# Retention heads: strips of one head between the attention steps of the former, key tiles from token 0, values centred by token

## The reference

```
k = k * RET_DK ** -0.5                       # 4 heads, RET_DK = 128, RET_DV = 256
scores = einsum(qc, kc) * intra              # intra[i, j] = gamma_h ** (i - j) where i >= j, else 0
out = einsum(scores, vc) + einsum(qc * q_decay, state)
ret = head_layer_norm(out)                   # over the 256 values of a head:
#   mu = mean(y); var = mean((y - mu) ** 2); (y - mu) * rsqrt(var + EPS)
ret = ret * silu(rg)
merged = g0 * (ret @ w_branch[0]) + g1 * (diff @ w_branch[1]) + g2 * (conv @ w_branch[2])
```

## Time and profile before

| | |
|---|---|
| median of 3 runs | 2200.36 us (2197.75 to 2200.51) |
| span of the profiled execution | 2196.6 us |
| TensorE busy | 2150.5 us (98%) |
| VectorE busy | 1150.0 us (52%) |
| ScalarE busy | 776.6 us (35%) |
| GpSimd busy | 51.3 us (2%) |
| chain that ended last | TensorE 93%, VectorE 4%, ScalarE 2% |

### The profile page before, as it was taken

One profiled execution on the slowest core, in us unless ns is written; L12 is line 12 of the kernel. 1 busy time (PEld: TensorE's weight loads), 2 busy tenths in 40 slices (PEclk: granted clock), 3 DMA queues, 4 the chain that ended last, 5 costly groups with the idle time before them and its releaser, 6 DMA issues.

```text
span 2196.6 us, 33725 instructions
## 1 busy us (share of the span) xinstructions
PE 2150.5 (98%) x13184; PEld 1851.5 (84%) x13184; DVE 1150.0 (52%) x1719; ACT 776.6 (35%) x1214; POOL 51.3 (2%) x79
## 2 busy tenths in 40 slices
PE   9999998999999999999999999999999989999998
PEld 8988994677888778888888888999999988889896
DVE  6553332443555645535445665457755556546365
ACT  4222221332344533323223466333433333222233
POOL 0000000000000000000000000012200000000000
PEclk9999999999999999999999999999999999999999
DMA  4232220132222132223222221231123222222222
GB/s 148 93 105 95 86 86 20 58 106 95 74 72 68 58 126 96 92 96 101 90 96 95 83 92 58 86 118 59 54 103 128 94 77 77 95 87 96 96 87 96
DMA packets 52966, 194.66 MB, mean 89 GB/s; under 512 B 6896, under 2 KB 7280, under 8 KB 52224
## 3 DMA queue, kind: packets, MB, share of 16 engines
q1 hardware_dynamic: 49248, 177.56, 24.6%
q10 hardware_dynamic: 2656, 12.41, 1.5%
q0 software_dynamic: 960, 3.24, 0.5%
HBM read 186.77 MB, written 6.42 MB: 88 GB/s over the span
## 4 chain that ended last, share of the span: by engine, by line
PE 93%; DVE 4%; ACT 2%; issue 1%; DMA 0%; DVEq 0%; ACTq 0%; SPq 0%
PE ps L1797 75%; PE ps L2356 5%; PE ps L2223 1%; PE ps L2013 1%; PE ps L2038 1%; PE ps L1972 1%; PE ps L1957 1%; PE ps L2288 1%; PE ps L2129 1%; DVE kk_r L1441 1%; PE ps L2052 1%; ACT kk L715 0%; ACT kk L716 0%; PE ps L2266 0%; PE ps L2110 0%
## 5 line engine op out<-in xcount | busy, mean ns | idle before, releaser
L406 ACT ACTIVATE wh<-wraw 128x1024 fp32r<-128x1024 f32 x330 | 348.2, 1055 | 834.4 <-PE ps L1797 725.5
L975 DVE TENSOR_TENSOR wl<-wraw,wh 128x1024 fp32r<-128x1024 f32 x330 | 403.4, 1223 | 144.9 <-ACT wh L406 138.0
L1797 PE MATMUL ps<-xh,wh 128*128 128x264 f32 (+1 forms) x2088 | 392.2, 333 | 9.7 <-ACT wh L406 5.7
L1797 PE MATMUL ps<-xh,wl 128*128 128x264 f32 (+1 forms) x2088 | 385.9, 330 | 0.0
L1797 PE MATMUL ps<-xl,wh 128*128 128x264 f32 (+1 forms) x2088 | 385.8, 330 | 0.0
L1797 PEld LDWEIGHTS ps<-xh,wh 128*128 128x128 f32 x2088 | 315.9, 189 | 51.8 <-ACT wh L406 4.6
L1797 PEld LDWEIGHTS ps<-xh,wl 128*128 128x128 f32 x2088 | 316.3, 188 | 38.2
L1797 PEld LDWEIGHTS ps<-xl,wh 128*128 128x128 f32 x2088 | 316.3, 188 | 38.2
L1797 PE MATMUL ps<-bh,wh 128*128 128x264 f32 (+1 forms) x1296 | 234.3, 325 | 3.9 <-DVE hf L1008 1.7
L1797 PE MATMUL ps<-bl,wh 128*128 128x264 f32 (+1 forms) x1296 | 230.9, 322 | 0.0
L1797 PE MATMUL ps<-bh,wl 128*128 128x264 f32 (+1 forms) x1296 | 230.6, 322 | 0.0
(11 more groups left out here) (420 smaller groups left out, 2030.1 us busy)
## 6 DMA issues: line engine op xcount, KB each, us to landing
wraw<-weights_dram SPq DMA_DIRECT2D x331, 512.0 KB, 3.5
hf<-tables_dram POOLq DMA_DIRECT2D x12, 264.0 KB, 3.0
res<-x_t_dram SPq DMA_DIRECT2D x4, 528.0 KB, 7.4
res<-x_t_dram ACTq DMA_DIRECT2D x1, 2112.0 KB, 9.1
res_dram<-res ACTq DMA_DIRECT2D x1, 2112.0 KB, 7.7
mrg_dram<-mrg ACTq DMA_DIRECT2D x1, 2112.0 KB, 7.3
mrg<-mrg_dram ACTq DMA_DIRECT2D x1, 2112.0 KB, 10.6
res<-res_dram ACTq DMA_DIRECT2D x1, 2112.0 KB, 16.5
```

Of the source, the lines that this page charges most:

```text
L406: nc.scalar.activation(wh[:, slot], wraw[:, slot], ACT.Copy).then_inc(hi_done, 1)
L975: nc.vector.tensor_tensor(wl[:, slot], wraw[:, slot], wh[:, slot].bitcast(F32), ALU.subtract)\
L1797: last = nc.tensor.matmul(o, w[:, slot, c, :], a[:, c, tok], start=(k == 0), stop=(k == len(steps) - 1))
```

## The change

- TensorE, VectorE and ScalarE each get one loop written out over 24 strips (`N_RET`) and what follows them. Head h's attention steps stand ahead of the strips 4h + 4 to 4h + 7: `scores`, then the turns of its two value strips and the sum of the former head's squares, then the products for each half. For head 3 these are gate strips.
- Weights come in that order: q, k and two v strips of a head, then the gates. q strips are over 512 tokens.
- Key tiles are tokens 0 to 127, and so on, with the last 16 as a fifth tile: 512, 400, 272, 144 and 16 queries.
- Values are centred once per token in `vt` (`centred_values`) ahead of the products, so outputs have mean 0: the mean matmuls and the subtraction on the outputs go. ScalarE squares straight from PSUM, VectorE adds the two squares, and one matmul sums them.
- Banks: strips 1 to 3 have banks 2 to 7; later ones over 528 tokens have banks 0 and 1, over 512 bank 0 or 1 by parity. `scores` use banks 2 to 4, the turns the same banks afterwards, products banks 5 and 6, the sum bank 7.
- Gates stay in `qq` till all heads are done, then silu, gating and parts follow within the last slots (`ret_silu`, `ret_gated`, `ret_parts`). The weight parts of the first `w_branch` strip of `ret_out` are made ahead (`ahead=True`).

The diff, cut:

```diff
+        RSTRIP, N_RET = START["ret_qkv"], 4 * RH + KC
+        def ret_width(j):
+            return SEQ if j >= 4 * RH or j % 4 == 0 else T
+        def ret_bank(j):
+            return 2 * j if 0 < j < 4 else j % 2 if ret_width(j) == SEQ else 0
+        def first_query(t):
+            return max(P * t - NM, 0)
+        def scores_ap(t):
+            return (ps[:, 2, :], ps[:, 3, 0:400], ps[:, 4, 0:272], ps[:, 4, 272:416], ps[0:NM, 4, 416:432])[t]
+        ret_silu = {21: (0, 1, 2), 22: (3, 4, 5), 23: (6,), 24: (7,)}
+        ret_gated = {22: (0, 1, 2), 23: (3, 4), 24: (5, 6), 25: (7,)}
+        ret_parts = {23: (0, 1, 2), 24: (3, 4), 25: (5, 6), 26: (7,)}
...
 ScalarE
+            for i in range(N_RET + 3):
+                if i <= N_RET:
+                    n = RSTRIP + i + 1
+                    split_hi(n, n // 2, n % 2)
+                h, step = divmod(i - 4, 4)
+                if step == 1 and 0 <= h < RH:
+                    for v in range(2):
+                        f = RDV * h + P * v
+                        act.wait_ge(vtr_done, 2 * h + v + 1)
+                        nc.scalar.activation(vt[:, 0:4, f:f + P], ps[:, 2 + v, :]..., ACT.Copy)
+                        act.wait_ge(vtr_done, 2 * h + 2)
+                        nc.scalar.activation(vt[0:NM, 4, f:f + P], ps[0:NM, 4, P * v:P * v + P], ACT.Copy)\
+                            .then_inc(vt_done, 1)
+                if step >= 2 and 0 <= h < RH:
+                    v = step - 2
+                    act.wait_ge(ro_ready, 2 * h + v + 1)
+                    if h and v == 0:
+                        act.wait_ge(rsum_done, h)
+                    nc.scalar.activation(kk[:, 2 * h + v, NM:T], ps[:, 5 + v, :], ACT.Copy)
+                    nc.scalar.activation(xrows[:, v, NM:T], ps[:, 5 + v, :], ACT.Square).then_inc(ro_copied, 1)
+                if step == 1 and 0 <= h - 1 < RH:
+                    w = h - 1
+                    act.wait_ge(rsum_done, w + 1)
+                    if w >= 2:
+                        act.wait_ge(r_scaled, 2 * (w - 1))
+                    root(xrows[:, 2 + w % 2, NM:T], ps[:, 7, :], 1.0 / RDV)
+                    if w == RH - 1:
+                        table_set(SILU)
+                for c in ret_silu.get(i, ()):
+                    n = RSTRIP + 4 * RH + c
+                    act.wait_ge(evicted[n % 2], n // 2 + 1)
+                    nc.scalar.activation(qq[:, c, NM:T], qq[:, c, NM:T], ACT.Silu).then_inc(rsilu_done, 1)
+                for c in ret_parts.get(i, ()):
+                    act.wait_ge(hf_ready, c + 1)
+                    hi_of(bh[:, c, NM:T], qq[:, c, NM:T])
...
 VectorE
+            def ret_evict(j):
...
+                if h >= RH:
+                    ins = scaled_by_root(qq[:, j - 4 * RH, NM:T], ret_ap(j), SEQ)
...
+                    if h:
+                        dve.wait_ge(vtr_done, 2 * (h - 1) + kind - 1)
+                    ins = scaled_by_root(two(tmp[:, kind - 2]), ret_ap(j), T)
+                ins.then_inc(evicted[n % 2], 1)
+            def centred_values(h):
+                dve.wait_ge(vt_done, 2 * h + 2)
+                f = slice(RDV * h, RDV * h + RDV)
+                nc.vector.tensor_reduce(stat[:, 0:4], vt[:, 0:4, f], AX, ALU.add)
+                link(nc.vector.tensor_reduce(stat[0:NM, 4:5], vt[0:NM, 4, f], AX, ALU.add))
+                nc.vector.scalar_tensor_tensor(out=vt[:, 0:4, f], in0=stat[:, 0:4].unsqueeze(2).to_broadcast([P, 4, RDV]),
+                                               scalar=-1.0 / RDV, in1=vt[:, 0:4, f], op0=ALU.mult, op1=ALU.add)
+                nc.vector.scalar_tensor_tensor(out=vt[0:NM, 4, f], in0=stat[0:NM, 4:5].to_broadcast([NM, RDV]),
+                                               scalar=-1.0 / RDV, in1=vt[0:NM, 4, f], op0=ALU.mult, op1=ALU.add)\
+                    .then_inc(centred, 1)
+            for i in range(N_RET + 3):
+                if 1 <= i <= N_RET:
+                    ret_evict(i - 1)
+                if i <= N_RET:
+                    n = RSTRIP + i + 1
+                    split_lo(n, n // 2, n % 2)
+                h, step = divmod(i - 4, 4)
+                if step == 0 and 0 <= h - 1 < RH:
+                    dve.wait_ge(ro_copied, 2 * h)
+                    nc.vector.tensor_tensor(xrows[:, 0, NM:T], xrows[:, 0, NM:T], xrows[:, 1, NM:T], ALU.add)\
+                        .then_inc(rsq_added, 1)
+                if step == 0 and 0 <= h < RH:
+                    masked_scores(h)
+                if step == 1 and 0 <= h < RH:
+                    centred_values(h)
+                if step == 2 and 0 <= h - 1 < RH:
...
+                        nc.vector.tensor_tensor(y, y, xrows[:, 2 + w % 2, NM:T], ALU.mult).then_inc(r_scaled, 1)
+                for c in ret_gated.get(i, ()):
...
+                for c in ret_parts.get(i, ()):
...
 TensorE
-            def mean(h):
...
+            def products(h, v):
+                pe.wait_ge(centred, h + 1)
+                if h:
+                    pe.wait_ge(ro_copied, 2 * (h - 1) + v + 1)
...
+            def ret_sums(h):
+                pe.wait_ge(rsq_added, h + 1)
+                if h:
+                    pe.wait_ge(root_ready, 1 + h)
+                nc.tensor.matmul(ps[:, 7, :], ones, xrows[:, 0, NM:T], start=True, stop=True).then_inc(rsum_done, 1)
+            for i in range(N_RET):
+                h, step = divmod(i - 4, 4)
+                if step == 0 and 0 <= h < RH:
+                    scores(h)
+                if step == 1 and 0 <= h < RH:
+                    turn_ret_values(h)
+                if step == 1 and 0 <= h - 1 < RH:
+                    ret_sums(h - 1)
+                if step >= 2 and 0 <= h < RH:
+                    products(h, step - 2)
+                n = RSTRIP + i
+                k = n - 1 if i >= 4 and T in (ret_width(i), ret_width(i - 1)) else n - 2
+                pe.wait_ge(evicted[k % 2], k // 2 + 1)
+                strip((n, n // 2, n % 2), "x", ret_width(i), bank=ret_bank(i), free=True)
```

More of the change, by code:

```diff
@@ L529, in splits_one @@
                 split_hi(*pos(B, 1))
[L531 to L546, removed]
@@ L1136, in branch_out @@
                         nc.vector.tensor_tensor(m, m, row(tmp[:, 0], n), ALU.add).then_inc(mrg_sum, 1)
+                first_then_loop(dve, KC, gate_and_branch)
                 n_sig += KC
[L1139 to L1145, removed]
@@ L1843, in strips @@
                         strip(pos(B, j, i), src, n, chunks=chunks)
-            def sum_rows(bank, rows, n=SEQ, squares=True):
-                nonlocal n_sq
-                for k in range(rows):
-                    pe.wait_ge(sq_ready, n_sq + 1)
-                    for tok, o in ([(slice(NM, T), ps[:, bank, :])] if n == SEQ else
-                                   [(slice(HALF * q, HALF * q + HALF), ps[:, bank + q, 0:HALF]) for q in range(2)]):
-                        last = nc.tensor.matmul(o, ones, tmp[:, n_sq % 2, tok], start=(k == 0), stop=(k == rows - 1))
-                    last.then_inc(sq_used, 1)
-                    n_sq += 1
             def strips_and_sums(B, src, n, ready, chunks=range(KC)):
@@ L1959, in scores, with turn_ret_values @@
+                if h:
+                    pe.wait_ge(vt_done, 2 * h)
+                for t in range(5):
+                    q0 = first_query(t)
+                    keys = qq[:, 4 + h, P * t:P * t + P] if t < 4 else qq[:, 4 + h, SEQ:T]
+                    ins = nc.tensor.matmul(scores_ap(t), keys, qq[:, h, NM + q0:T] if t < 4 else qq[:, h, SEQ:T],
+                                           start=True, stop=True)
+                    if t in (0, 1, 4):
                         ins.then_inc(rz_ready, 1)
-            def products(h):
+            def turn_ret_values(h):
+                n = RSTRIP + 4 * h + 3
+                pe.wait_ge(evicted[n % 2], n // 2 + 1)
@@ L1993, in _ @@
-            mean(RH - 1)
-            strip(pos(START["ret_gate"], 0), "x", SEQ)
-            sum_rows(2 * ((RH - 1) % 2) + 1, 2)
-            strip(pos(START["ret_gate"], 1), "x", SEQ)
-            with pe.Fori(1, KC // 2) as i:
-                for j in range(2):
-                    strip(pos(START["ret_gate"], j, i), "x", SEQ)
+                    for kb in range(4):
+                        nc.tensor.transpose(ps[:, 2 + v, P * kb:P * kb + P], tmp[:, v, P * kb:P * kb + P], ident)
+                    nc.tensor.transpose(ps[0:NM, 4, P * v:P * v + P], tmp[:, v, SEQ:T], ident).then_inc(vtr_done, 1)
```

208 lines of the change are left out of this document (56 added, 152 removed).

## The result

The changed kernel takes 2162.9 us (median of 4 runs, 2162.6 to 2163.3) against 2199.6 for the kernel before (4 runs); the ratio is 0.9835, with a 95% interval of 0.9823 to 0.9847. It is faster, by 1.65%. My forecast was 2169.9 with a range of 2164 to 2181: the direction holds and nothing new waits, as I had said, but I had priced the attention work too high and started the sum from the wrong base, and the time lies 1.1 us under the range.

The account below looks back on a forecast made before the run. TensorE was taken to bound the kernel, leading the chain for 93% of the span. Strips 142.2, attention 41.4 and mixing 2.8 made a 186.4 us stretch against 216.90, 30.5 less: 2169.9 us, range 2164 to 2181.

Parts of the forecast that it names:

- nothing new waits: Retention stretch: all moved work is hidden under strips, 30.5 us less, 2169.9 us; chance 0.70.
- lower bound: Centring on VectorE in the turn slot: 3.4 us as ordinary operations, hidden, no cost.
- heaviest gate slots: Gate slots of 5.57 us: VectorE has 5.9 us of work, 0.3 to 0.7 late, carried over; nothing waits.
- Case 2: Centring at its upper bound: products wait at the head of their slot, 2173.1 us; chance 0.13.
- Case 3: Evictions late in the one-bank order: thirteen strips pay 0.8 us each, 10.4 us, 2180.3; chance 0.08.
- Case 4: Another engine paces the slots, so TensorE's saving becomes waiting: 2191 us; chance 0.05.
- Case 5: Slower: granted clock falls in the mixed stretch; 2313 us if throughout; chance 0.04 with everything else of this sign.
- the base: Time the saving was subtracted from: the runs' median 2200.36 us, taken as 3.8 outside the span of 2196.6.
- the attention term: Retention heads: scores and products 33.0 us, value turns 5.0, sums 3.4; together 41.4 us.
- mixing: Strips behind attention steps: 0.20 us more for twelve, 0.1 each for four, together 2.8 us.
- my own signs: Signs of being right included: stretch about 186 us, clock 1.00, mixed strips 5.8 to 6.0, products and scores 2.75.

Follow-up runs that it names:

- e5: Changed kernel with each head's values centred twice, the second time changing them by next to nothing: 2170.26 us, ratio 0.9867.
- e4: Changed kernel with both halves of a head's products in front of the same strip: 2166.45 us, ratio 0.9850.
- e2: Kernel before with key tiles from token 0 and nothing else: 2190.82 us, ratio 0.9961.
- e3: Kernel before with all of TensorE's new work (tiles, centred values, squares from PSUM, one sum) in the old order, no strips between attention: 2180.17 us, ratio 0.9912.
- e7: Changed kernel without the early weight parts for the first w_branch strip of ret_out: 2167.11 us, ratio 0.9852.
- e6: Changed kernel with the five key tiles' scores in reverse order, 16-wide first, masks waiting for all five: 2162.67 us, ratio 0.9835.
- e1: Changed kernel run once more with no edit, beside the kernel before: 2163.04 us, ratio 0.9834.
- e9: Kernel before with the new TensorE work in the old order, and ScalarE making a head's root ahead of the next head's squares: 2176.37 us, ratio 0.9897.

## Why the prediction was right and where it was off

**Right: that nothing new waits.** The forecast's likeliest case was that nothing new waits. It is what happened: no wait of TensorE in the stretch, evictions, masks, copies and roots all under strips. The centring took its lower bound, 3.1 us against 3.4. In the heaviest gate slots VectorE is not 0.3 to 0.7 us late, as I had said, but waits 0.18 for the strip. It falls behind only after them, and begins to evict the first gates strip of `ret_out` 1.75 us after the next strip has started; nothing waits for it. The Trainium skill (VectorE: DVE Perf Modes, the perf-mode tier table, with the fixed term of the section on the TRN2 errata) had let me estimate 1.22 us for the wide reduction; by that rule, the trace agrees, with 1220 ns.

**Rivals.** Case 2 did not occur; e5 shows what it would have cost and that the cover was 1.3 us in head 0. Case 3 did not occur; its price of 0.8 per strip was too low by the 0.27 of the strip behind (e4). Case 4: VectorE is busy for 14.3 of 32.1 us of a head. Case 5: the clock stayed at 1.00 in the mixed stretch, transposes included. In the block order (e2, e3), and behind the longest waits that I put in (e5, e7), it fell, and the work behind took 1.4 to 2.0 us longer.

**Off: the size.** Forecast and result differ by 7.0 us: 2.0 in the base, 4.6 in the stretch, 0.4 elsewhere. The step that failed is the attention term, "Scores and products make 12 x 2.75 = 33.0" and the turns with it: 41.4 us forecast, 37.8 measured, with 0.20 us in rows of the diff stage that the sum charged a second time as mixing. It took both this and the base to leave the range: either one alone would have left the time inside it, by under 3 us. Of my own signs two failed by it: the stretch took 181.8 us and not about 186, scores and products 2.38 and 2.55 and not 2.75.
- The base, 2.0 us. I subtracted from the median shown, 2200.36, and read its 3.8 us over the span as time outside it. It is 1.8, which puts the profiled execution at 2198.4. From there the same sum gives 2167.9.
- The attention term, 3.6 of the stretch's 4.6 us. "Scores and products make 12 x 2.75": the row of 2.43 for four product tiles came from a place behind a 16-wide matmul and so had the 0.20 in it that I then charged again as the price of mixing. Behind a strip they take 2.23: 8 x 0.2 = 1.6. The scores' fifth tile has 16 weight columns and not 128, a load of 94 ns, and not 182, which by the counting below is worth 0.17 (no run changed it alone): with the same 0.20 this makes 4 x 0.37 = 1.5. The turns, read behind a narrow matmul too, 4 x 0.14 = 0.6; unrounded, 3.6 together. e2, e4 and e6 show the cause: the same matmuls take 2.23 or 2.43 by what stands in front, and the 0.20 moves when the order does.
- The rest of the stretch: mixing 2.4 and not 2.8 (behind the 512-wide sum a strip pays 0.01), strips 5.80 and 5.56 in place of 5.82 and 5.57, 0.4. By these figures the stretch is 12 x 5.80 + 13 x 5.56 + 4 x 2.38 + 8 x 2.55 + 4 x 1.10 + 4 x 0.86 + 2.4 = 182.0 against the measured 181.8.
- 0.6 us beyond the stretch, less 0.2 between the profiled run and the median. Most of the 0.6 lies in 35 us of a late stage, 1750 to 1785 us in after, whose mean clock is 0.95, and 0.90 in the same work of before. The profiled execution of e1, the same kernel as after, has 0.90 there and a span 0.9 us longer, so this is scatter.

**The account of the gain.** By e9, 22.3 of 35.5 us come from less TensorE work (tiles, means, sums of squares) and the waits for squares that go with it. The rest of the diff, the interleaving above all, brings 13.2: the waits around the last value turn, for a mask, for a root, before the gates and before `ret_out`, 1.75 + 0.84 + 1.53 + 3.81 + 1.13 = 9.1; the clock behind the 3.8 us wait, 3.3 - 1.9 = 1.4; the q strips, 1.0; the rest, under 2 us, I did not take apart (0.27 behind each of the five other waits, as in e4, would be an estimate of 1.4 of it). Which share falls to which idea depends on the order in which they are added, and no run has the old attention work between the strips, so that the interleaving by itself was not measured. I had not tried to say which of the two ideas carries the gain.

**The rule behind the 0.20.** An fp32 matmul shows two records, each with a load of its own. What the rows of e2, e4 and e6 and those above have in common: a load of 128 columns (0.19 us) is hidden behind a pass longer than itself, and not behind one of 144 or 16 columns. Counting for each pass the larger of its columns (512 take 0.43 us) and the load that follows gives 2.58 us for scores with the strip's first load and 2.74 for products; measured are 2.38 + 0.20 and 2.55 + 0.20. For the reversed scores it gives 2.64, where 2.58 were measured, so it is good to 0.06. The Trainium skill (TensorE: Matmul & The Clock Gate, LDWEIGHTS) states that load time goes with columns, not rows. By that rule, the trace agrees, 182 ns for 16 x 128 against 94 for 128 x 16. An estimate from that page's figure of P / 1.2 would be 107 and 13 ns; both loads took longer here.

## What to carry to other kernels

A duration that a chain of waits shows includes what the instruction in front leaves exposed: before a row from another stage goes into a sum, look at what stands in front of it there, and charge that once. Take the base of a sum from the same execution as its rows, its span and the constant outside it. And where TensorE paces, first look for work that can leave it: here that was worth 22 of 36 us in the old order, and the rest of the change took the waits and the clock's falls behind them.

## What was not expected of the hardware

- A wait of TensorE costs more than itself, even at a granted clock of 1.00: the work behind it took 0.27 us longer, a strip 6.07 and not 5.80 (e4), products 2.50 and not 2.23 (three times in e5).
- Behind waits of 1.9 to 2.7 us the granted clock also fell, and work behind them took 1.4 to 2.0 us longer in all (e3: 3.87 for 2.43; e5: 4.20 for 2.23; e7: 7.22 for 5.56). Behind 1.53 us in e9 it did not (2.47).
- The length of one wait does not tell whether the clock falls. Of three waits of 1.6 us for squares in e2 one had a fall behind it, and the same three in before had none. Two waits of 0.8 to 0.9 us ahead of the first scores had a fall behind them in e2 (6.91 us for 20 records), and none in e3 (5.22).
- The kernels with such waits scatter more: e2's runs lie over 4.6 us, those of the changed kernel over 1. That this is the clock is argued from the mean clocks of e2's runs; one of them alone was profiled.
